# First two modulation chunks issued ahead of the parameter loads, a fifth expert slot, 8 KB down runs and another quad order, in a four-layer float32 transformer kernel

## The reference

```python
def moe_swiglu(u, router_w, w1, w3, w2):          # layer 2: 8 experts, inner width 2816
    ...
    top_vals, top_idx = lax.top_k(logits, TOP_K)  # TOP_K = 2
    ...
        return (jax.nn.silu(xb @ w1[e]) * (xb @ w3[e])) @ w2[e]
...
def grouped_moe(x, router_w, router_b, w_gate, w_up, w_down):   # layers A and B: 16 experts, inner width 512
    ...
    for e in range(N_EXPERTS_2):
        h = jax.nn.silu(xt @ w_gate[e]) * (xt @ w_up[e])
        out = out + combine[:, e:e + 1] * (h @ w_down[e])
```

## Time and profile before

| | |
|---|---|
| median of 3 runs | 2384.19 us (2379.34 to 2388.86) |
| the profiled execution | 2381.78 us, of which its span is 2380.1 us |
| TensorE busy | 2103.5 us, 88% of the span |
| DMA | 644.22 MB, 271 GB/s over the span |
| mean granted TensorE clock | 0.95 |

### The profile page before, as it was taken

How to read it: one execution, slowest core, us unless ns; L and a number is a source line. 1 busy time by engine, 2 the same in 40 slices (tenths; PEclk the granted TensorE clock), 3 DMA queues, 4 the chain that set the end, 5 groups by cost and what they waited for, 6 DMA issues and landing times. The chain is left out here.

```text
span 2380.1 us, 29544 instructions
## 1 busy us (share of the span) xinstructions
PE 2103.5 (88%) x12194; PEld 951.6 (40%) x12194; DVE 500.0 (21%) x1274; ACT 377.9 (16%) x878; POOL 143.8 (6%) x275
## 2 busy tenths in 40 slices
PE   3999998999999899999999988987778879767787
PEld 1574553444677343222222222254423328432232
DVE  2133751000159220000000100112301032131113
ACT  1012432000341321000000000122111010110101
POOL 2000000000000100000000000000001000000000
PEclk9999999999999999999999998997889999888999
DMA  9232348442673579999999999840899972079993
GB/s 309 74 106 71 142 168 291 159 159 89 230 265 129 221 287 365 409 402 399 409 404 397 409 406 399 317 144 0 321 418 417 417 292 89 36 311 416 417 417 119
DMA packets 209303, 644.22 MB, mean 271 GB/s; under 512 B 11507, under 2 KB 42699, under 8 KB 192779
## 3 DMA queue, kind: packets, MB, share of 16 engines
q1 hardware_dynamic: 163883, 470.16, 51.7%
q0 software_dynamic: 45280, 172.09, 18.5%
HBM read 641.15 MB, written 1.05 MB: 270 GB/s over the span
## 5 line engine op out<-in xcount | busy, mean ns | idle before, releaser
L1344 PE MATMUL bank<-ring,wide 128*32 128x512 f32 x3520 | 423.1, 610 | 34.7 <-DMA ring<-in_l_moe_w 33.0
L1381 PE MATMUL bank<-dreg,RB 128*32 128x512 f32 x2592 | 319.4, 612 | 37.4 <-DMA dreg<-in_w_down 37.4
L1344 PEld LDWEIGHTS bank<-ring,wide 128*32 128x32 f32 x3520 | 109.5, 111 | 295.1 <-issue 268.7
L1329 PE MATMUL bank<-ring,wide 128*32 128x512 f32 x1664 | 191.7, 610 | 28.8 <-DMA ring<-in_w_up 27.5
L954 PE MATMUL bank<-wide,ring 128*128 128x256 f32 x832 | 181.8, 381 | 0.6 <-ACT wide L1784 0.6
L2903 DVE TENSOR_TENSOR H<-SG,bank 128x256 f32<-128x256 f32 x82 | 34.5, 421 | 684.9 <-ACT SG L2017 684.9
L1381 PEld LDWEIGHTS bank<-dreg,RB 128*32 128x32 f32 x2592 | 79.4, 112 | 221.8 <-issue 220.6
L954 PEld LDWEIGHTS bank<-wide,ring 128*128 128x128 f32 x832 | 158.3, 191 | 24.0 <-issue 2.2
L944 PE MATMUL bank<-ring,wide 128*128 128x512 f32 x352 | 157.7, 607 | 1.0 <-DMA ring<-in_w_kv 0.8
L1253 PE MATMUL bank<-ring,wide 128*128 128x512 f32 x352 | 154.6, 592 | 0.9 <-ACT wide L1784 0.9
L2017 ACT ACTIVATE SG<-bank 128x256 f32<-128x256 f32 x82 | 31.4, 383 | 694.2 <-PE bank L1344 403.0
(11 more groups left out here) (441 smaller groups left out, 1607.8 us busy)
## 6 DMA issues: line engine op xcount, KB each, us to landing
ring<-in_l_moe_w SPq DMA_DIRECT2D x128, 1024.0 KB, 16.7
dreg<-in_l_moe_w POOLq DMA_DIRECT2D x88, 1024.0 KB, 10.0
ring<-in_w_gate SPq DMA_DIRECT2D x64, 1024.0 KB, 11.9
ring<-in_w_up SPq DMA_DIRECT2D x64, 1024.0 KB, 15.2
dreg<-in_w_down POOLq DMA_DIRECT2D x64, 1024.0 KB, 14.2
ring<-in_l_mod_w SPq DMA_DIRECT2D x24, 2048.0 KB, 8.2
ring<-in_l_moe_w SPq DMA_DIRECT2D x32, 768.0 KB, 12.2
ring<-in_l_ffn_w SPq DMA_DIRECT2D x22, 1024.0 KB, 10.1
```

The source lines that it names most:

```text
L1329: mm = pe.matmul(banks[r % 2][32 * g:32 * g + 32, :].rearrange("p (w n) -> p w n", w=2), tokens_of(m.order[i][0], c, k), w, start=k == 0, ...
L1344: mm = pe.matmul(banks[r % 3][32 * g:32 * g + 32, :].rearrange("p (w n) -> p w n", w=2), tokens_of(m.order[i][0], c, k), quads[:, s, :, k ...
L1381: mm = pe.matmul(banks[4 + 2 * m.lane(m.unit(m.order[i][0])) + h][32 * g:32 * g + 32, :], HQ[:, r % 4, j, 32 * q:32 * q + 32], dring[:, i ...
```

## The change

The diff has four parts.

**1. Start.** `mod0_0` and `mod0_1` are issued before the 15 small loads. X and TOK come after these.

**2. Fifth slot.** A fifth slot for halves lies in `RS`, for the first 20 halves of layers A and B (`SLOTS2`). Its first load waits for update 5 of X (7 in layer B), when the norm has read its parameter rows. The rows that stood in RS are loaded again behind the slot's last use (`rows_again`): four rows in A, where three were loaded ahead of the first down loads before and one much earlier, and two in B, which were loaded ahead of layer B's projections before.

**3. Down runs.** `(j p)` becomes `(p j)` in `down_loads`, for all three expert parts: a partition reads two neighbouring rows of w2, 8 KB in one run, where it read two separate runs of 4 KB. `multiply` reads and writes H's columns in the matching order.

**4. Quad order.** The order of the quads in `MOE1` is another. Chunks per block of the quads, from the tenth on, were 2, 3, 3, 2, 3, (2,2,1,1), 3, 3, 1, 3, 1, (1,3,3,3), 3, and are now (2,3,3,3), 3, 2, 3, 3, 2, 3, 3, (2,1,1,1), 3, 3, 1, 1. The quads whose up weights come in runs of 3 KB and 1 KB, where an expert ends within the quad, go from four to five; those in runs of 2 KB stay two.

```diff
@@ MOE1 = QuadMoe(... @@
-               [0, 0, 1, 0, 1, 0, 0, 1, 0, 1, 0, 0, 1, 0, 1, 0, 0, 1, 0, 1, 2, 0])
+               [0, 0, 1, 0, 1, 0, 0, 1, 0, 2, 0, 1, 0, 0, 1, 0, 0, 1, 0, 0, 1, 1])
@@ def slot(self, q, h) @@
-        return self.halves.index((q, h)) % RING
+        n = self.halves.index((q, h))
+        return n % SLOTS2 if n < 4 * SLOTS2 else n % RING
...
+        half_slots = [pairs[:, s, :, :, :] for s in range(RING)] + [carve(RSf, 0, 2, KC // 2, NCH)]
@@ def down_loads @@
-                eng.dma_start(dring[:, s, :, :], w2(e)[f, :].rearrange("(j p) n -> p j n", p=P)).then_inc(sem(f"moe_down_in{s}"), 16)
+                eng.dma_start(dring[:, s, :, :], w2(e)[f, :].rearrange("(p j) n -> p j n", p=P)).then_inc(sem(f"moe_down_in{s}"), 16)
@@ block.sync @@
+            for s, n in enumerate(("mod0_0", "mod0_1")):
+                sp.dma_start(ring[:, s, :, :], wsrc[n]).then_inc(sem(f"chunk_in{s}"), 16)
             row0 = 0
...
-            load("mod0_0")
             sp.dma_start(X[:, :, :], ...
-            load("mod0_1")
@@ def expert_loads @@
                     if n < RING:
                         slot_free(slot)
+                    elif n == RING:
+                        sp.wait_ge(sem("x_updated"), updated)
@@ block.gpsimd @@
-                           (1, 0, A["ln1_g_2"][0], D), (2, 0, A["ln1_b_2"][0], D), (3, 0, A["ln2_g_2"][0], D)])
+                           (1, 0, A["ln1_g_2"][0], D), (2, 0, A["ln1_b_2"][0], D)])
...
-            rows_after(5, [(0, 0, A["ln2_b_2"][0], D), (1, 0, A["ln1_g_2"][1], D), (2, 0, A["ln1_b_2"][1], D)])
-            down_loads(pool, MOEA, lambda e: A["w_down_2"][0, e], range(MOEA.blocks))
+            def rows_again(m, loads):
+                r, h = m.last_in(RING)
+                passed = ("upped_low", "upped")[h]
+                pool.wait_ge(sem(f"moe_{passed}"), m.before[passed] + r + 1)
+                for s, a in loads:
+                    pool.dma_start(RS[:, s, :], row(a, D)).then_inc(sem("params_in"), 16)
+            def rows_lead(m):
+                return [i for i in range(RING, m.blocks) if m.done_in(i - RING) + 2 > m.last_in(RING)[0]][0]
+            pool.wait_ge(sem("x_updated"), 5)
+            lead = rows_lead(MOEA)
+            down_loads(pool, MOEA, lambda e: A["w_down_2"][0, e], range(lead))
+            rows_again(MOEA, [(3, A["ln2_g_2"][0]), (0, A["ln2_b_2"][0]), (1, A["ln1_g_2"][1]), (2, A["ln1_b_2"][1])])
+            down_loads(pool, MOEA, lambda e: A["w_down_2"][0, e], range(lead, MOEA.blocks))
...
-            rows_after(6, [(3, 0, A["ln2_g_2"][1], D), (0, 0, A["ln2_b_2"][1], D)])
             pool.wait_ge(sem("x_updated"), 7)
-            down_loads(pool, MOEB, lambda e: A["w_down_2"][1, e], range(MOEB.blocks))
+            down_loads(pool, MOEB, lambda e: A["w_down_2"][1, e], range(lead))
+            rows_again(MOEB, [(3, A["ln2_g_2"][1]), (0, A["ln2_b_2"][1])])
+            down_loads(pool, MOEB, lambda e: A["w_down_2"][1, e], range(lead, MOEB.blocks))
@@ def multiply(r) @@
-                    i = dve.tensor_tensor(H[:, r % 2, :], SG[:, r % 2, :], banks[r % up_banks][:, FSTEP:NCH], ALU.mult)
+                    apart = lambda v: v.rearrange("q (p j) -> q j p", j=2)
+                    i = dve.tensor_tensor(H[:, r % 2, :].rearrange("q (j p) -> q j p", j=2), apart(SG[:, r % 2, :]),
+                                          apart(banks[r % up_banks][:, FSTEP:NCH]), ALU.mult)
```

More of the change, by code:

```diff
@@ L40 @@
 RING = 4
+SLOTS2 = RING + 1
 QUAD = 32
@@ L85, in counts @@
         n |= {"all_placed": 4 * TT, "down_done": self.blocks, "quarter": 0}
-        n |= {f"up_in{s}": self.loaded(*self.halves[len(self.halves) - RING + s]) for s in range(RING)}
+        n |= {f"up_in{s}": self.loaded(*self.in_slot(s)[-1]) for s in range(SLOTS2)}
         n |= {f"down_in{s}": 16 * len(range(s, self.blocks, RING)) for s in range(RING)}
@@ L96, in slot, with in_slot, last_in @@
     def slot(self, q, h):
-        return self.halves.index((q, h)) % RING
+        n = self.halves.index((q, h))
+        return n % SLOTS2 if n < 4 * SLOTS2 else n % RING
+    def in_slot(self, s):
+        return [a for a in self.halves if self.slot(*a) == s]
+    def last_in(self, s):
+        q, h = self.in_slot(s)[-1]
+        return max(self.pair_rounds(q)), h
     def loaded(self, q, h):
-        n = self.halves.index((q, h))
-        return sum(2 * 16 * len(self.runs(p)) for p, _ in self.halves[n % RING:n + 1:RING])
+        here = self.in_slot(self.slot(q, h))
+        return sum(2 * 16 * len(self.runs(p)) for p, _ in here[:here.index((q, h)) + 1])
     def in_pair(self, i):
@@ L243, in counts @@
         n |= {"all_placed": len(self.gathers) * TT, "down_done": self.blocks, "quarter": 3 * self.quads, "upped_low": 0}
-        n |= {f"up_in{s}": self.quarters_in(self.quads - 1) for s in range(RING)}
+        n |= {f"up_in{s}": self.quarters_in(self.quads - 1) if s < RING else 0 for s in range(SLOTS2)}
         n |= {f"down_in{s}": 16 * len(range(s, self.blocks, RING)) for s in range(RING)}
@@ L667, in _ @@
             sp.dma_start(pack[0:TAPS * KC - P, 3, :], dw[P:TAPS * KC, :]).then_inc(sem("packed"), 16)
-            holder = [None] * RING
+            holder = ["mod0_0", "mod0_1", None, None]
             def slot_free(s):
@@ L731, in expert_loads @@
                             rows = w(expert_at(sp, m, known, p)).rearrange("(p k) n -> p k n", p=P)
-                            sp.dma_start(pairs[:, slot, i, :, at:at + width], rows[:, 4 * h:4 * h + 4, lo:lo + width]).then_inc(
+                            sp.dma_start(half_slots[slot][:, i, :, at:at + width], rows[:, 4 * h:4 * h + 4, lo:lo + width]).then_inc(
                                 sem(f"moe_up_in{slot}"), 16)
@@ L1327, in up @@
                                 q, odd = m.in_pair(i)
-                                w = pairs[:, m.slot(q, half), :, k % 4, odd * FSTEP:(odd + 1) * FSTEP]
+                                w = half_slots[m.slot(q, half)][:, :, k % 4, odd * FSTEP:(odd + 1) * FSTEP]
                                 mm = pe.matmul(banks[r % 2][32 * g:32 * g + 32, :].rearrange("p (w n) -> p w n", w=2),
@@ L3037, in _ @@
             step(dve.memset(sguT[64:P, :, 0:64], 0.0))
-            dve.wait_ge(sem("params_in"), 16 * 8)
+            dve.wait_ge(sem("params_in"), 16 * 7)
             V = UV[:, :, 1, :]
@@ L3087, in _ @@
             for l, name in ((0, "A"), (1, "B")):
-                projected(name, 8 if l == 0 else 11)
+                projected(name, 7 if l == 0 else 11)
                 group_router(name)
```

9 lines of the change are left out of this document (5 added, 4 removed).

## The result

The kernel after takes 2367.15 us (median of 6 runs, 2362.49 to 2369.71) against 2380.74 us for the kernel before in the same comparison. The ratio is 0.9936, 95% interval [0.9923, 0.9949]: 13.6 us faster by the medians, 12 to 18 us by the interval, where 33.9 were forecast. The profiled execution took 2369.41 us, its span is 2367.7.

A forecast was written before the change was run, and what follows sets the result against it. The prediction took DMA bytes to bound the expert stretches (978 us). Gains of 4.7 (start), 11.7 (down runs), 15.0 (quad order) and 2.5 (fifth slot) sum to 33.9 us, giving 2350 us, range 2339 to 2368.

The forecast's parts named there:

- The rival at 2368: Middle of the odd layer's experts: TensorE needs 5% more than 370 us, so 18 us come back; chance 0.10.
- the rivals on long packets that bring little, or are slow: 8 KB down runs on q0: little gain, 2362 us, chance 0.11; or costlier than two of 4 KB, chance 0.04.
- 2.3 and 2.2 us: Experts of layers A and B: gains from 8 KB down runs, at 0.095 us for each of 24 and 23 loads.
- the time is bytes over rate: Byte-bound expert stretches, 978 us: time is bytes over rate, then the tail from last up load to last product.
- the slower case: Down loads on q0: 8 KB runs cost more than two of 4 KB; 2433 us at 400 ns; chance 0.04.
- my 40.2, 19.0 and 6.2: Odd layer's end: old tail 40.2 us, new tail 19.0, less 5.2 for two loads ahead and 1.0 for short runs.
- the 9 us that I called free: Start: the small loads, with `packed`, may land 9 us later at no cost.
- The rival that the small loads hold the start up: Start: small loads are held in issue, so it gives -1.5 us instead of 4.7; 2356 us, chance 0.10.
- the 0.9 that I took off: Start: 0.9 us deducted for the small loads' packets, which now lie within the stream of chunks.
- The sum is 0: Layer A's experts: the fifth slot's 2.1 MB and four reloaded rows, 2.1 MB, leave no gain.
- a net 2.5: Layer B's experts: the fifth slot saves 5.0 us, its two reloaded rows cost 2.5, leaving 2.5.
- A's stretch shortens only by the runs: Sign for layer A's experts: only the longer down runs shorten the stretch, by 2.3 us.

The follow-up runs named there:

- start_order: Kernel before with the new start and the new quad order, without long runs and fifth slot: 2366.69 us, ratio 0.9936.
- no_fifth_short_ab: Kernel before with new start, new quad order and 8 KB down runs in layer 2's experts alone, no fifth slot: 2359.56 us, ratio 0.9915.
- long_odd: Kernel before with 8 KB down runs in layer 2's experts alone: 2379.32 us, ratio 0.9975.
- long_ab: Kernel before with 8 KB down runs in the experts of layers A and B alone: 2389.43 us, ratio 1.0027.
- order_alone: Kernel before with the new quad order alone: 2373.52 us, ratio 0.9966.
- ctx_behind: Kernel before with only the load of the context TOK moved behind mod0_2 and mod0_3: 2384.88 us, ratio 1.0011.
- long_three: Kernel before with 8 KB down runs everywhere and at most three down loads ahead instead of four in A and B: 2386.81 us, ratio 1.0017.

## Why the prediction was wrong

It named 2350 us and 0.85 for a gain over 0.5%. The sign was right and 2367.15 lies just within the range, but the gain was 13.6 us instead of 33.9. That it lies in the range is no sign for the mechanism: against the sum, the gain of part 3 is 17.0 us smaller, that of part 4 is 5.9 and that of part 2 is 1.4, and that of part 1 is 4.1 larger. The rival at 2368, TensorE as the bound, has the number by luck; its cause is out, as shown under part 4. By the terms of the sum:

**Part 3, forecast 11.7, measured -5.3: the step that failed.** In layer 2 the stage held: 6.7 and 7.0 us in two kernels against 7.2, and 7.1 from start_order to no_fifth_short_ab. Over 923 to 1508 us q0 carried the same 79.70 MB in 34.3% of 16 x 585 us before and in 33.0% in long_odd, 7.6 us less on each engine. A long packet comes to 317.5 ns and two short ones to 330.0, where I had 315.5 and 327.4 from the earlier trace rows: the rivals on long packets that bring little, or are slow, are out. The Trainium skill's rule quoted in the prediction ("DMA: Bandwidth & Descriptors", section "Why small descriptors are slow (HBM only)") gave 1.1% for this; the trace has 3.8%. What failed is the step "2.3 and 2.2 us" for A and B. I priced a longer packet by its own duration alone and took order for given, since in a stretch bound by bytes "the time is bytes over rate". In layers A and B it also matters which bytes come first: with the long runs the last up load came 1.5 us later in long_ab's layer A, and TensorE's one long idle before it was followed by products that took 1.7 us more at the lower clock. The earlier trace rows already showed the two queues side by side with unequal packets, and I read only the durations from them. Cost: 7.1 us instead of a gain of 4.5. No rival had it; the slower case looked for a slow packet, not for a fast one in the wrong place.

**Part 4, forecast 15.0, measured 9.1: a term mis-sized, the old tail.** I counted 40.2 us from "the up loads end near 1513", where the DMA's rate falls. But the last two up loads were issued by 1498.3 and took a median of 19.6 us to land. The DMA issues of the kernel before in 1495 to 1520 us (count, KB each, median us to landing):

```profile
ring<-in_l_moe_w SPq DMA_DIRECT2D x2, 1024.0 KB, 19.6
```

By the trace's landing times the last of them took 23.2 us and landed at 1519.2, not near 1513. In these 6 us the rate was about half, and the load was not done. Counted from there the old tail is 34.0 us, in which TensorE, behind as it was, did not notice the late landing. In order_alone it does (same view, then TensorE's timeline from the last up products on):

```profile
ring<-in_l_moe_w SPq DMA_DIRECT2D x2, 1024.0 KB, 22.7
```

```profile
1526.49 1.92 PE L1344 MATMUL bank<-ring,wide 128*32 128x512 f32 x16 [1.46 <-DMA ring<-in_l_moe_w]
...
1531.11 2.78 PE L1381 MATMUL bank<-dreg,RB 128*32 128x512 f32 x24 [0.56 <-ACT RB L2024]
1539.11 1.94 PE L1381 MATMUL bank<-dreg,RB 128*32 128x512 f32 x8 [5.22 <-DMA dreg<-in_l_moe_w]
...
1542.87 3.87 PE L1403 MATMUL bank<-T 64*128 64x512 f32 x8 [0.78 <-ACT T L2031]
```

From the landing at 1526.4 to the end at 1546.7 it is 20.3 us; I had 19.0 for that, with the same steps. The gain is 34.0 - 20.3 - 4.8 (the landing, 679.3 us into the stage instead of 674.5) = 8.9. That sum must come out; what counts are its terms, against my 40.2, 19.0 and 6.2. The 6.2 had an error of its own: two thirds of a load and the last one are 1.67 loads, not 1.5, so that 1.75 MB or 4.3 us go ahead, not 5.2. The kernel after ends layer 2 in the same manner:

```profile
1509.80 3.64 PE L1378 MATMUL bank<-ring,wide 128*32 128x512 f32 x16 [8.15 <-DMA ring<-in_l_moe_w]
...
1515.91 1.92 PE L1378 MATMUL bank<-ring,wide 128*32 128x512 f32 x16
...
1530.96 3.87 PE L1437 MATMUL bank<-T 64*128 64x512 f32 x8 [0.78 <-ACT T L2065]
```

TensorE catches up so well with the small quads that it now idles 8.15 us for the late third quarter. The DMA share stays at 1.03 from 920 to 1508 us, too, and TensorE's waits for layer 2's up loads fell only from 33.0 to 21.6 us. The rival "TensorE bounds the middle" is out.

**Part 1, forecast 4.7, measured 8.8: mis-sized the other way.** The timeline of the start, after:

```profile
0.94 1.08 SPq L668 DMA_DIRECT2D ring<-in_l_mod_w  x2
...
12.77 2.19 SPq L793 DMA_DIRECT2D TOK<-in_ctx  x1
15.00 10.60 SPq L699 DMA_DIRECT2D ring<-in_l_mod_w  x2
...
22.35 1.00 PE L1072 MATMUL bank<-ident,T 128*128 128x128 f32 x4 [22.35 <-DMA T<-in_l_conv_dw_w]
26.53 5.22 PE L999 MATMUL bank<-ring,CB 128*32 128x512 f32 x32 [3.19 <-DVE CB L2425]
34.04 1.92 PE L999 MATMUL bank<-ring,CB 128*32 128x512 f32 x16 [2.29 <-DMA ring<-in_l_mod_w]
...
39.47 1.92 PE L999 MATMUL bank<-ring,CB 128*32 128x512 f32 x16 [1.60 <-DMA ring<-in_l_mod_w]
```

The parameters do become late, as foreseen: `packed` at 22.35, beyond the 9 us that I called free, and the first product 2.5 us later than before. Yet the fourth starts at 39.47, not 43. The rival that the small loads hold the start up is out. These are the windows to 12 us and to 40 us (DMA share and GB/s at the end), first before, then after:

```profile
0.00:12.00 12.00, 0.99 (x4) 0.64 (x4) 1.25 (x7) 0.00 (x0) 10.38 (x27) 1.00 0.42 76
12.00:40.00 28.00, 7.29 (x32) 1.29 (x32) 9.00 (x24) 3.60 (x5) 4.69 (x13) 1.00 1.04 371
...
0.00:12.00 12.00, 0.00 (x0) 0.00 (x0) 0.63 (x3) 0.00 (x0) 10.39 (x27) 1.00 0.84 258
12.00:40.00 28.00, 10.57 (x76) 4.17 (x80) 11.18 (x30) 4.90 (x8) 4.71 (x13) 1.00 1.05 361
```

By 12 us 3.1 MB have moved instead of 0.9, and from then on the engines are full in both kernels. The 2.2 MB are 5.9 us at 371 GB/s, about the 5.6 us by which I let the stream begin earlier, without the 0.9 that I took off. The rest was missing in the sum: when the third chunk lands, the engines have moved 12.2 MB before and 10.9 MB after, so 1.3 MB of other loads no longer come ahead of it. Which they are, and why, stays open. SP's shorter hold in TOK's issue, 2.19 us instead of 15.67, lets SP issue the third chunk at 15.00 instead of 24.05, but by the landings in ctx_behind's section that is not shown to be worth anything. One execution also misled: its fourth product at 47.92 is below the mean of the seven with the old order of loads (46.2 to 50.7, mean 48.6).

**Part 2, forecast 2.5, measured 1.1 with no difference to be told.** "The sum is 0" for A held (249.7). For B I had a net 2.5, and nothing came (250.0). With the rows out of the way A and B gain 4.0 and 2.0 us, and without slot nothing of the kind is there (249.5, 250.0). This fits a slot whose gain the rows take back, in A too, where I had called them even. A kernel with the rows moved and nothing else was not run.

**The signs** that I named: q0's packets got shorter per byte, 317.5 ns for 8 KB, and the odd layer runs at 406 GB/s. From the last up load's landing to the odd layer's last scatter it is 20.1 us (1514.7 to 1534.8). Layer A's idle stayed near 4 us (153 GB/s in 1688 to 1694), layer B's fell to 6.7 (20 GB/s in 2103 to 2110) where I had 9. "A's stretch shortens only by the runs" was the sentence that the profile refuted, with 255.9 instead of 249.7.

## What to carry to other kernels

Where two queues feed one engine, a packet's size can also be that queue's weight, as it was in these traces. Before lengthening one queue's runs, compare the share of bytes that it gets with the share that the consumer needs, and look at which load each wait is for. Count a tail from the landing of the last load that is waited for, not from the fall of the transfer rate. And after a change of several parts, run each alone: here one of four ate 5 us, and keeping it only where it helped gave some 7 back. Before a delay in issuing a load is called a cause, look whether the load would have landed earlier.

## What the runs showed of the hardware

- The turns are exact: 1045 to 1044 packets in 28 us with 8 and 4 KB, 495 to 494 in 17 us with both at 8 KB. The rate is 417 and 424 GB/s in the two windows, so the turns cost no bandwidth.
- The last loads of a full stretch spread out. The last up load of layer 2 needed 23.2 us to land before and 25.6 us in order_alone, and the rate had fallen below 300 GB/s some 6 us before the landing.
- SyncE can be held in the issue of a load, 13.5 to 19.1 us for TOK's with the old start. Moved behind two more chunks, the hold fell on the chunks (20.14 us for three), and TOK's own was 6.11. In these traces the hold did not delay the chunk behind it: that landed 5.4 us after the load ahead of it each time.
- After one idle piece of 10.5 to 11.8 us, 32 products took 5.11 to 5.89 us in all six stages with long runs (long_three apart), where they took 3.64 in layer A before. In long_ab the granted clock was 0.71 over the idle piece and 0.67 over the products.
